# Down projection of a residual block in f32: one unit in six turns of each sweep by seven block products

## The chip, the cores and the metric

One core of a Trainium2 chip runs the whole kernel. The time is device microseconds of one execution. The kernel before takes 1611.67 us (median of 3 runs, 1611.58 to 1612.26).

## The reference, cut to what matters

```python
def conv_ffn(h, w_up, conv_w, w_down):
    ...
    return (jax.nn.gelu(gate, approximate=True) * val) @ w_down

def reference(x, ...):
    ...
    x = x + rms_norm(mix, ln_post_mix)
    h2 = rms_norm(x, ln_pre_ffn)
    x = x + rms_norm(conv_ffn(h2, w_up, conv_w, w_down), ln_post_ffn)
    return x
```

All is float32. There are 256 tokens, a model width of 2048 and an inner width of 8192, so the down projection is a product of 256x8192 with 8192x2048.

## The kernel before, in words

Every weight matrix is streamed once from HBM. A float32 product is made of three passes on TensorE: each operand is split into a rounded part `hi` (type fp32r) and the rest `lo`, and hi·hi, hi·lo and lo·hi are added in PSUM. ScalarE (ACT) makes `hi` with a copy that rounds, VectorE (DVE) makes `lo` with a subtraction, TensorE (PE) multiplies, SyncE (SP) issues the loads. Each engine runs a list of instructions that is written out by hand, in order, and semaphores tie the lists together.

The weights pass through `raw`, four slots of 128x2048 numbers (1 MB each, one load per slot, `load`, L282), and from there, in halves of 128x1024, through two rings of four places, `w_hi` and `w_lo` (`split`: L381 on ACT, L726 on DVE). Eight halves are a turn. In the down projection a half is one k tile (128 rows of `w_down`) by 1024 columns. Its 128x256 activations, a row of `ffT`, are split at the same time into `xs` (`split_xs`: L392 on ACT, L732 on DVE). `half_b` (L1320) then makes 12 matmuls of it: two tiles of 128 tokens, three passes, two column blocks of 512. There are two sweeps, one for each 1024 columns of the output, with 64 k tiles in 8 turns of 8 halves each. Sweep 0 adds up in PSUM banks 4 to 7, sweep 1 in banks 0 to 3. In the code the first turn of a sweep is written out and the others are a hardware loop (`down_turn`, L691 on ACT and L1191 on DVE); on PE the last turn is written out too, and in sweep 1 its last four halves are made by `last_halves` (L1334), tile by tile, so that the norm of the first tokens starts earlier.

What holds the order together around the change: ACT may write half h of turn m once `half_used` has reached 8m+h-3, that is when PE is through with the half that lay in the same ring place. DVE waits for `hi_ready` of the same half, PE for `lo_ready`. The load of slot s waits until `lo_ready` has reached 8m+2s-6, so slot 3 is loaded again when the whole turn before has been split.

At the boundary of the sweeps, in turn 0 of sweep 1, ACT squares the four finished banks of sweep 0 and DVE takes them out of PSUM (`sweep_out`). `actT`, 64 KB of each partition, holds the activations of the projections before and is used in the down projection only for what the squares write.

## Time and profile before

| | |
|---|---|
| median of 3 runs | 1611.67 us |
| the profiled execution, its own time | 1612.33 us |
| its span, first to last instruction | 1610.6 us |
| PE busy | 1600.2 us, 99% of the span |
| DVE busy | 1127.9 us, 70% |
| ACT busy | 791.1 us, 49% |
| DMA, share of 16 engines over the span | 61% |
| mean granted TensorE clock | 0.999 |

The span counts from the first to the last instruction; the execution's own time holds 1.7 us more around it. Busy times are of instructions; a matmul's time in the trace is longer than the distance to the next one, since they overlap. "PEld" is the load of the stationary operand, which runs beside the matmuls. An idle time is named with the engine and the line that ended it.

### The profile page before, as it was taken

What the parts mean: (1) busy time and instruction counts of PE and PEld (TensorE: products, weight loads), DVE (VectorE), ACT (ScalarE), POOL (GpSimd) and SP (SyncE); (2) the same over time, 40 slices, a digit from 0 to 9 for tenths busy, and PEclk for the clock granted to TensorE, in tenths of its full rate; (3) what the DMA queues carried; (4) which work ended last, traced back from release to release, by engine and by line L of the source; (5) the groups of instructions that cost most, each with busy time, mean ns of one, the idle gap of its engine ahead of it and who ended that gap; (6) DMA issues with size and microseconds to landing.
All of it is one profiled execution on the core that took longest, in us unless ns stands there. A gap on an engine that the chain in (4) does not pass through costs nothing.

```text
span 1610.6 us, 24829 instructions
## 1 busy us (share of the span) xinstructions
PE 1600.2 (99%) x8716; PEld 1384.2 (86%) x8716; DVE 1127.9 (70%) x1578; ACT 791.1 (49%) x1045; POOL 1.9 (0%) x12
## 2 busy tenths in 40 slices
PE   9999999999999999999999999999999999999998
PEld 7888888888888888888888888888888888888886
DVE  6556667677766787777777777777777755565555
ACT  6544544456555644444444444444444545554453
POOL 0000000000000000000000000000000000000000
PEclk9999999999999999999999999999999999999999
DMA  9885455556676465655655556556556666666662
GB/s 368 264 224 188 158 183 167 172 156 209 195 254 198 146 205 188 196 183 183 198 190 185 185 185 202 182 184 194 185 192 187 217 196 187 199 188 196 195 187 100
DMA packets 234788, 312.96 MB, mean 194 GB/s; under 512 B 5344, under 2 KB 209792, under 8 KB 233856
## 3 DMA queue, kind: packets, MB, share of 16 engines
q1 hardware_dynamic: 230912, 306.44, 59.6%
q10 hardware_dynamic: 3840, 6.05, 1.5%
q8 instruction: 23, 0.38, 0.1%
q14 instruction: 13, 0.11, 0.0%
HBM read 309.58 MB, written 2.88 MB: 194 GB/s over the span
## 4 chain that ended last, share of the span: by engine, by line
PE 99%; DMA 0%; DVE 0%; ACT 0%; SPq 0%; issue 0%; DVEq 0%
PE ps L1237 44%; PE ps L1328 26%; PE ps L1241 23%; PE ps L1376 3%; PE ps L1341 1%; PE ps L1252 1%; DMA raw<-in_w_in_dram 0%; PE ps L1257 0%; PE ps L1452 0%; PE ps L1470 0%; PE ps L1445 0%; PE ps L1460 0%; PE ps L1517 0%; DVE arena L1213 0%; PE ps L1281 0%; PE ps L1269 0%
## 5 line engine op out<-in xcount | busy, mean ns | idle before, releaser
L729 DVE TENSOR_TENSOR w_lo<-raw,w_hi 128x1024 fp32r<-128x1024 f32 x566 | 681.7, 1222 | 248.9 <-ACT w_hi L389 246.8
L389 ACT ACTIVATE w_hi<-raw 128x1024 fp32r<-128x1024 f32 x565 | 585.9, 1055 | 509.2 <-PE ps L1237 259.6
L1237 PE MATMUL ps<-actT,w_hi 128*128 128x512 f32 x3072 | 719.7, 390 | 0.0
L1237 PEld LDWEIGHTS ps<-actT,w_hi 128*128 128x128 f32 x3072 | 569.3, 188 | 115.5 <-issue 1.7
L1241 PEld LDWEIGHTS ps<-actT,w_lo 128*128 128x128 f32 x3072 | 383.2, 191 | 9.7 <-issue 1.4
L1241 PE MATMUL ps<-actT,w_lo 128*128 128x256 f32 x3072 | 388.9, 283 | 0.0
L1328 PE MATMUL ps<-w_hi,xs 128*128 128x512 f32 x1216 | 325.3, 389 | 0.0
L1328 PEld LDWEIGHTS ps<-w_hi,xs 128*128 128x128 f32 x1216 | 228.2, 188 | 47.3
L1328 PE MATMUL ps<-w_lo,xs 128*128 128x512 f32 x608 | 187.3, 389 | 0.0
L735 DVE TENSOR_TENSOR xs<-arena,xs 128x256 fp32r<-128x256 f32 x160 | 68.0, 425 | 169.4 <-ACT w_hi L389 169.1
L395 ACT ACTIVATE xs<-arena 128x256 fp32r (+1 forms) x160 | 66.7, 417 | 208.0 <-PE ps L1328 196.9
L1328 PEld LDWEIGHTS ps<-w_lo,xs 128*128 128x128 f32 x608 | 114.1, 188 | 23.8
L1141 DVE SCALAR_TENSOR_TENSOR arena<-arena,convw 128x256 f32<-128x256 f32 x256 | 106.9, 480 | 0.1
L740 DVE TENSOR_TENSOR arena<-ps,arena 128x512 f32<-128x512 f32 (+1 forms) x106 | 72.5, 684 | 1.6 <-ACT arena L402 1.6
L402 ACT ACTIVATE arena<-ps 128x512 f32<-128x512 f32 x106 | 61.4, 579 | 2.9 <-PE ps L1257 1.4
L1129 DVE TENSOR_TENSOR arena<-arena,rrow 128x512 f32<-128x512 f32 x64 | 44.3, 692 | 6.5
L1137 DVE TENSOR_SCALAR arena<-arena,convw 128x256 f32<-128x256 f32 x128 | 39.5, 351 | 8.9 <-DVE arena L1129 0.2
L1376 PE MATMUL ps<-w_hi,actT 128*128 128x512 f32 x128 | 32.5, 396 | 0.7 <-ACT w_hi L389 0.7
L1376 PEld LDWEIGHTS ps<-w_hi,actT 128*128 128x128 f32 x128 | 24.3, 192 | 6.4 <-issue 1.3
L568 ACT ACTIVATE arena<-ps 128x512 f32<-128x512 f32 x8 | 4.8, 597 | 35.3 <-PE ps L1460 35.3
L1171 DVE TENSOR_TENSOR arena<-arena 128x512 f32 (+1 forms) x32 | 22.0, 687 | 0.1
L674 ACT ACTIVATE arena<-arena 128x512 f32<-128x512 f32 x32 | 19.9, 622 | 1.1 <-DVE arena L1141 1.1
(132 smaller groups left out, 411.9 us busy)
## 6 DMA issues: line engine op xcount, KB each, us to landing
raw<-in_w_up_dram SPq DMA_DIRECT2D x128, 1024.0 KB, 5.5
raw<-in_w_down_dram SPq DMA_DIRECT2D x64, 1024.0 KB, 5.5
raw<-in_w_in_dram SPq DMA_DIRECT2D x58, 1024.0 KB, 5.2
raw<-in_w_o_dram SPq DMA_DIRECT2D x16, 1024.0 KB, 5.6
raw<-in_w_a_out_dram SPq DMA_DIRECT2D x8, 1024.0 KB, 5.2
raw<-in_w_b_out_dram SPq DMA_DIRECT2D x8, 1024.0 KB, 5.2
arena<-in_x_dram SPq DMA_DIRECT2D x1, 2048.0 KB, 17.3
arena<-in_x_dram ACTq DMA_DIRECT2D x2, 1024.0 KB, 6.6
```

The costliest lines, as they stand in the source:

```text
L389: act.activation(w_hi[:, h % RING, :], raw[:, h // 2, h % 2 * HALF:(h % 2 + 1) * HALF], ACT.Copy)\
L395: act.activation(xs[:, h % RING, 0, :], src, ACT.Copy)
L402: act.activation(lo_part, ps[:, bank:bank + 2, S:2 * S], ACT.Copy).then_inc(copied, 1)
L729: dve.tensor_tensor(w_lo[:, h % RING, :], raw[:, h // 2, h % 2 * HALF:(h % 2 + 1) * HALF], w_hi[:, h % RING, :].bitcast(F32), ALU.subtract ...
L735: dve.tensor_tensor(xs[:, h % RING, 1, :], src, xs[:, h % RING, 0, :].bitcast(F32), ALU.subtract)
L740: dve.tensor_tensor(dst, ps[:, bank:bank + 2, 0:S], lo_part, ALU.add).then_inc(summed, 1)
L1129: dve.tensor_tensor(src[:, :, 2:], src[:, :, 2:], rrow[:].unsqueeze(1).broadcast_to([P, 2, S]), ALU.mult)\
L1141: dve.scalar_tensor_tensor(out=dst[:, a, :], in0=src[:, a, i:i + S], scalar=w(i, a), in1=dst[:, a, :], op0=ALU.mult, op1=ALU.add).then_inc ...
L1237: return pe.matmul(ps[:, bank + c, :], w_hi[:, h % RING, at:at + P], actT[:, k, :, :].rearrange("p a s -> p (a s)"), start=start, stop=stop)
L1241: return pe.matmul(ps[:, bank + c, 0:S], w_lo[:, h % RING, at:at + P], actT[:, k, 0, :], start=start, stop=stop)
L1328: ins = pe.matmul(ps[:, bank + 2 * t + c, :], xpart[:, tokens], wpart[:, slot, c * 512:(c + 1) * 512], start=(first and xpart is x_hi and ...
L1376: ins = pe.matmul(ps[:, 4 + 2 * t + c, :], xpart[:, t * P:(t + 1) * P], wpart[:, slot, c * 512:(c + 1) * 512], start=(k == 0 and xpart is ...
```

## The change

In turns 1 to 6 of each sweep the last two halves (k tiles 8i+6 and 8i+7 of the turn, slot 3 of `raw`) are no longer multiplied with 24 matmuls. The 256x256 activations and the 256x1024 weights are taken as 2x2 blocks, and Strassen's scheme in Winograd's form makes the product of seven block products, each of three passes: 21 matmuls (`seven_products`, L1697 of the new kernel). The blocks and their sums are split into `hi` and `lo` in `forms`, which lies in `actT`, and in a small new tile `a_parts`; `convw`, `rrow` and `yn[sweep]` hold the sums.

- DVE makes seven sums (`sum_forms`) behind half 4 and the `lo` parts in eight subtractions (`rest_of_forms`) behind half 5. ACT rounds in `round_given` (four instructions) behind half 4 and in `round_sums` (four) behind half 5. ACT and DVE do not split halves 6 and 7 in these turns.
- PE waits for all of it (`lo_ready` at 8m+8) before the first of the 21 matmuls. Three of the seven products go into the banks of the sweep's sum (one each), four (P1, P5, P6, P7) into the other four banks, where they add up over the six turns. All 21 give `half_used` its 2 at the end.
- In the last turn of a sweep ACT copies P1 out of PSUM behind half 1 (`copy_p1`), and DVE adds P5, P6 and P7 to it behind half 3 (`sum_products`, four instructions). Sweep 0: the result is added to the sweep's banks by DVE in turn 0 of sweep 1, before ACT's squares, which now read it from SBUF and wait for it (`c_summed`); the multiplication by the gain moves behind half 5. Sweep 1: ACT rounds the result (`round_u`, behind its half 3), DVE makes the rest (`rest_of_u`, behind its half 5), and PE adds both to its banks with 8 matmuls by the identity (`add_products`) between half 3 of the last turn and `last_halves`.
- After a turn with seven products ACT may write halves 0 to 3 at other counts of `half_used` (`FREED`): 8m-3, 8m-2, 8m-5, 8m-4 in place of 8m-3 to 8m.
- The loops of ACT, DVE and PE now cover turns 2 to 5; turns 0, 1, 6 and 7 are written out.
- PE's waits for free banks move: `summed` from the start of sweep 1 to the start of turn 1 of sweep 0; new ones are `u_summed` at the start and `c_summed` at turn 1 of sweep 1.

The diff, cut (indentation taken off, empty lines left out):

```diff
+forms = actT[:].rearrange("p k a s -> p (k a s)")
+B1, B2, BT, BLK = 0, 512, 1536, 512
+b_hi, b_lo = forms[:, 0:7 * BLK], forms[:, 7 * BLK:14 * BLK]
+s_hi, s_lo = forms[:, 7168:7680], forms[:, 7680:8192]
+a_parts = sb("a_parts", [P, 2, 3 * P], F32R)
+a_hi, a_lo = a_parts[:, 0, :], a_parts[:, 1, :]
+s123 = convw[:].rearrange("p i t -> p (i t)")
+s4 = rrow[:, 0:P]
+u_hi, u_lo, ident_r = forms[:, 0:2048], forms[:, 2048:4096], forms[:, 4096:4096 + P]
...
+SUMS, HALVES_HI = 7, 7
+FREED = (-3, -2, -5, -4)
+def forms_at(sweep, i):
+    return (FF // P // 8 - 2) * sweep + i - 1
...
+def round_given(m, i):
+    act.wait_ge(raw_landed[3], 16 * m + 16)
+    act.wait_ge(half_used, 8 * m)
+    act.activation(b_hi[:, B2:BT], raw[:, 3, 2 * BLK:4 * BLK], ACT.Copy).then_inc(form_hi, 1)
+    act.activation(b_hi[:, B1:B2], raw[:, 3, 0:BLK], ACT.Copy).then_inc(form_hi, 1)
+    act.activation(a_hi[:, 0:S], ffT[:, 8 * i + 7, :], ACT.Copy).then_inc(form_hi, 1)
+    act.activation(a_hi[:, S:S + P], ffT[:, 8 * i + 6, 0:P], ACT.Copy).then_inc(form_hi, 1)
+def round_sums(sweep, i):
+    n = forms_at(sweep, i)
+    act.wait_ge(form_summed, SUMS * n + 2)
+    act.activation(b_hi[:, BT:BT + 2 * BLK], yn[sweep][:, 0, :], ACT.Copy).then_inc(form_hi, 1)
+    act.wait_ge(form_summed, SUMS * n + 6)
+    act.activation(s_hi[:, 0:3 * P], s123, ACT.Copy).then_inc(form_hi, 1)
+    act.activation(s_hi[:, 3 * P:4 * P], s4, ACT.Copy).then_inc(form_hi, 1)
+    act.wait_ge(form_summed, SUMS * n + 7)
+    act.activation(b_hi[:, BT + 2 * BLK:BT + 4 * BLK], yn[sweep][:, 1, :], ACT.Copy).then_inc(hi_ready, 2)
+def copy_p1(sweep, m):
+    act.wait_ge(half_used, 8 * m)
+    act.activation(yn[sweep][:, 0, 0:BLK], ps[:, 4 * sweep, :], ACT.Copy).then_inc(u_copied, 1)
+def round_u():
+    act.activation(ident_r, ident[:], ACT.Copy)
+    act.wait_ge(u_summed, 8)
+    for t in range(T):
+        act.activation(u_hi[:, t * SW:(t + 1) * SW], yn[1][:, t, :], ACT.Copy).then_inc(u_rounded, 1)
+def down_turn(sweep, i, with_forms=False, behind_forms=False, first=False, last=False):
     m = i + (N_DOWN // 8 + sweep * (FF // P // 8))
     if sweep == 0:
         act.wait_ge(ff_done, 4 * i + 4)
-    for h in range(8):
-        split_xs(m, h, ffT[:, 8 * i + h, :])
+    for h in range(6 if with_forms else 8):
+        split_xs(m, h, ffT[:, 8 * i + h, :], free=FREED[h] if behind_forms and h < RING else None)
         if first and sweep == 0 and h == 3:
             copy_out(G_END - 1, 2, N_DOWN)
             gelu_of(FF // GC - 1)
         if first and sweep == 1 and h == 3:
-            act.wait_ge(half_used, N_DOWN + FF // P)
             for t in range(T):
-                square(ps[:, 4 + 2 * t:6 + 2 * t, :], actT[:, 2 * t:2 * t + 2, :, :], SWEEP_FFN + t)
+                act.wait_ge(c_summed, t + 1)
+                square(yn[0][:, t, :], actT[:, 2 * t:2 * t + 2, :, :], SWEEP_FFN + t)
+        if with_forms and h == 4:
+            round_given(m, i)
+        if with_forms and h == 5:
+            round_sums(sweep, i)
+        if last and h == 1:
+            copy_p1(sweep, m)
+        if last and sweep == 1 and h == 3:
+            round_u()
+turns = FF // P // 8
 down_turn(0, 0, first=True)
 act.wait_ge(ff_done, FF // GC)
 act.dma_start(gain2, ln_post_ffn.partition_broadcast(P)).then_inc(small["gain2"], 16)
-with act.Fori(1, FF // P // 8) as i:
-    down_turn(0, i)
-load_root_table(2)
-down_turn(1, 0, first=True)
-with act.Fori(1, FF // P // 8) as i:
-    down_turn(1, i)
+for sweep in range(2):
+    if sweep == 1:
+        load_root_table(2)
+        down_turn(1, 0, first=True)
+    down_turn(sweep, 1, with_forms=True)
+    with act.Fori(2, turns - 2) as i:
+        down_turn(sweep, i, with_forms=True, behind_forms=True)
+    down_turn(sweep, turns - 2, with_forms=True, behind_forms=True)
+    down_turn(sweep, turns - 1, behind_forms=True, last=True)
...
+def sum_forms(sweep, m, i):
+    n = SUMS * forms_at(sweep, i)
+    quarters = raw[:, 3, :].rearrange("p (a b c) -> p a b c", a=2, b=2)
+    t13, t2, t4 = two(yn[sweep][:, 0, :]), yn[sweep][:, 1, 0:BLK], yn[sweep][:, 1, BLK:2 * BLK]
+    b21, b22 = raw[:, 3, 2 * BLK:3 * BLK], raw[:, 3, 3 * BLK:4 * BLK]
+    a11, a21 = ffT[:, 8 * i + 6, 0:P], ffT[:, 8 * i + 6, P:S]
+    a12, a22 = ffT[:, 8 * i + 7, 0:P], ffT[:, 8 * i + 7, P:S]
+    s1, s2, s3 = (s123[:, q * P:(q + 1) * P] for q in range(3))
+    dve.wait_ge(raw_landed[3], 16 * m + 16)
+    dve.tensor_tensor(s1, a21, a22, ALU.add).then_inc(form_summed, 1)
+    dve.tensor_tensor(t13, quarters[:, :, 1, :], quarters[:, 0, :, :], ALU.subtract).then_inc(form_summed, 1)
+    dve.wait_ge(form_summed, n + 1)
+    dve.tensor_tensor(s2, s1, a11, ALU.subtract).then_inc(form_summed, 1)
+    dve.tensor_tensor(s3, a11, a21, ALU.subtract).then_inc(form_summed, 1)
+    dve.wait_ge(form_summed, n + 2)
+    dve.tensor_tensor(t2, b22, yn[sweep][:, 0, 0:BLK], ALU.subtract).then_inc(form_summed, 1)
+    dve.wait_ge(form_summed, n + 3)
+    dve.tensor_tensor(s4, a12, s2, ALU.subtract).then_inc(form_summed, 1)
+    dve.wait_ge(form_summed, n + 5)
+    dve.tensor_tensor(t4, b21, t2, ALU.subtract).then_inc(form_summed, 1)
+def rest_of_forms(sweep, m, i):
+    n = HALVES_HI * forms_at(sweep, i)
+    def rest(lo, full, hi):
+        dve.tensor_tensor(lo, full, hi.bitcast(F32), ALU.subtract).then_inc(form_lo, 1)
+    dve.wait_ge(form_hi, n + 1)
+    rest(b_lo[:, B2:BT], raw[:, 3, 2 * BLK:4 * BLK], b_hi[:, B2:BT])
+    dve.wait_ge(form_hi, n + 2)
+    rest(b_lo[:, B1:B2], raw[:, 3, 0:BLK], b_hi[:, B1:B2])
+    dve.wait_ge(form_hi, n + 3)
+    rest(a_lo[:, 0:S], ffT[:, 8 * i + 7, :], a_hi[:, 0:S])
+    dve.wait_ge(form_hi, n + 4)
+    rest(a_lo[:, S:S + P], ffT[:, 8 * i + 6, 0:P], a_hi[:, S:S + P])
+    dve.wait_ge(form_hi, n + 5)
+    rest(b_lo[:, BT:BT + 2 * BLK], yn[sweep][:, 0, :], b_hi[:, BT:BT + 2 * BLK])
+    dve.wait_ge(form_hi, n + 6)
+    rest(s_lo[:, 0:3 * P], s123, s_hi[:, 0:3 * P])
+    dve.wait_ge(form_hi, n + 7)
+    rest(s_lo[:, 3 * P:4 * P], s4, s_hi[:, 3 * P:4 * P])
+    dve.wait_ge(hi_ready, 8 * m + 8)
+    dve.tensor_tensor(b_lo[:, BT + 2 * BLK:BT + 4 * BLK], yn[sweep][:, 1, :],
+                      b_hi[:, BT + 2 * BLK:BT + 4 * BLK].bitcast(F32), ALU.subtract).then_inc(lo_ready, 2)
+def sum_products(sweep):
+    u = yn[sweep]
+    p5, p6, p7 = (ps[:, 4 * sweep + q, :] for q in (1, 2, 3))
+    dve.wait_ge(u_copied, sweep + 1)
+    dve.tensor_tensor(u[:, 0, BLK:SW], p6, u[:, 0, 0:BLK], ALU.add).then_inc(u_summed, 1)
+    dve.wait_ge(u_summed, 4 * sweep + 1)
+    dve.tensor_tensor(u[:, 1, 0:BLK], p7, u[:, 0, BLK:SW], ALU.add).then_inc(u_summed, 1)
+    dve.tensor_tensor(u[:, 0, BLK:SW], p5, u[:, 0, BLK:SW], ALU.add).then_inc(u_summed, 1)
+    dve.wait_ge(u_summed, 4 * sweep + 2)
+    dve.tensor_tensor(u[:, 1, BLK:SW], p5, u[:, 1, 0:BLK], ALU.add).then_inc(u_summed, 1)
+def rest_of_u():
+    for t in range(T):
+        dve.wait_ge(u_rounded, t + 1)
+        dve.tensor_tensor(u_lo[:, t * SW:(t + 1) * SW], yn[1][:, t, :],
+                          u_hi[:, t * SW:(t + 1) * SW].bitcast(F32), ALU.subtract).then_inc(u_rest, 1)
+def down_turn(sweep, i, with_forms=False, first=False, last=False):
     m = i + (N_DOWN // 8 + sweep * (FF // P // 8))
-    for h in range(8):
+    for h in range(6 if with_forms else 8):
         split_xs(m, h, ffT[:, 8 * i + h, :])
         if first and sweep == 0 and h == 3:
             value_half(FF // GC - 1)
             product(FF // GC - 1)
         if first and sweep == 1 and h == 3:
+            dve.wait_ge(half_used, N_DOWN + FF // P)
+            for t in range(T):
+                dve.tensor_tensor(two(yn[0][:, t, :]), ps[:, 4 + 2 * t:6 + 2 * t, :], two(yn[0][:, t, :]),
+                                  ALU.add).then_inc(c_summed, 1)
+        if first and sweep == 1 and h == 5:
             dve.wait_ge(small["gain2"], 16)
             for t in range(T):
-                sweep_out(4, t, yn[0][:, t, :], gain2[:, 0:SW], sq_done, 5 * T + t + 2)
+                dve.wait_ge(sq_done, 5 * T + t + 2)
+                dve.tensor_tensor(yn[0][:, t, :], yn[0][:, t, :], gain2[:, 0:SW], ALU.mult).then_inc(sw_out, 1)
+        if with_forms and h == 4:
+            sum_forms(sweep, m, i)
+        if with_forms and h == 5:
+            rest_of_forms(sweep, m, i)
+        if last and h == 3:
+            sum_products(sweep)
+        if last and sweep == 1 and h == 5:
+            rest_of_u()
...
+def seven_products(m, c_bank, p_bank, first=False, last=False):
+    def a_given(at):
+        return a_hi[:, at:at + P], a_lo[:, at:at + P]
+    def a_sum(q):
+        return s_hi[:, q * P:(q + 1) * P], s_lo[:, q * P:(q + 1) * P]
+    def b(at):
+        return b_hi[:, at:at + BLK], b_lo[:, at:at + BLK]
+    pe.wait_ge(lo_ready, 8 * m + 8)
+    for (x_hi, x_lo), (y_hi, y_lo), bank, alone in (
+            (a_given(S), b(B1), p_bank, True),
+            (a_given(0), b(B2), c_bank, False),
+            (a_sum(3), b(B2 + BLK), c_bank + 1, False),
+            (a_given(P), b(BT + 3 * BLK), c_bank + 2, False),
+            (a_sum(0), b(BT), p_bank + 1, True),
+            (a_sum(1), b(BT + 2 * BLK), p_bank + 2, True),
+            (a_sum(2), b(BT + BLK), p_bank + 3, True)):
+        pe.matmul(ps[:, bank, :], x_hi, y_hi, start=(first and alone), stop=False)
+        pe.matmul(ps[:, bank, :], x_hi, y_lo, start=False, stop=False)
+        ins = pe.matmul(ps[:, bank, :], x_lo, y_hi, start=False, stop=(last and alone))
+    ins.then_inc(half_used, 2)
+def add_products():
+    pe.wait_ge(u_rest, T)
+    for bank in range(4):
+        for part in (u_hi, u_lo):
+            pe.matmul(ps[:, bank, :], ident_r, part[:, bank * BLK:(bank + 1) * BLK], start=False, stop=False)
 for sweep in range(2):
-    bank = 4 - 4 * sweep
+    bank, p_bank = 4 - 4 * sweep, 4 * sweep
     m = N_DOWN // 8 + sweep * turns
+    def turn_of_seven(i, first=False, last=False):
+        b_turn(i + m, bank, range(6))
+        seven_products(i + m, bank, p_bank, first, last)
     if sweep == 1:
+        pe.wait_ge(u_summed, 4)
+    b_turn(m, bank, range(8), first=True)
+    if sweep == 0:
         pe.wait_ge(summed, G_END)
-    b_turn(m, bank, range(8), first=True)
-    with pe.Fori(1, turns - 1) as i:
-        b_turn(i + m, bank, range(8))
+    else:
+        pe.wait_ge(c_summed, T)
+    turn_of_seven(1, first=True)
+    with pe.Fori(2, turns - 2) as i:
+        turn_of_seven(i)
+    turn_of_seven(turns - 2, last=True)
     b_turn(m + turns - 1, bank, range(8) if sweep == 0 else range(4), last=True)
+add_products()
 last_halves(N_END // 8 - 1)
```

**Where the instructions move.** DVE, turn 1 of sweep 0 (`w_lo` of half 5, the eight rests, and the first half of the next turn); before, this stretch held halves 5, 6 and 7, each of these two rows:

```order
L735 TENSOR_TENSOR xs<-arena,xs 128x256
L729 TENSOR_TENSOR w_lo<-raw,w_hi 128x1024 [waits hi_ready]
L734 REGISTER_ALU
L735 ISA [waits hi_ready]
L735 TENSOR_TENSOR xs<-arena,xs 128x256
L729 TENSOR_TENSOR w_lo<-raw,w_hi 128x1024 [waits hi_ready]
```

Now:

```order
L1278 TENSOR_TENSOR arena<-raw,arena 128x512 [waits form_summed]
L802 TENSOR_TENSOR xs<-arena,xs 128x256 [waits hi_ready]
L796 TENSOR_TENSOR w_lo<-raw,w_hi 128x1024 [waits hi_ready]
L1285 TENSOR_TENSOR actT<-raw,actT 128x1024 [waits form_hi]
L1285 TENSOR_TENSOR actT<-raw,actT 128x512 [waits form_hi]
L1285 TENSOR_TENSOR a_parts<-arena,a_parts 128x256 [waits form_hi]
L1285 TENSOR_TENSOR a_parts<-arena,a_parts 128x128 [waits form_hi]
L1285 TENSOR_TENSOR actT<-arena,actT 128x1024 [waits form_hi]
L1285 TENSOR_TENSOR actT<-convw,actT 128x384 [waits form_hi]
L1285 TENSOR_TENSOR actT<-rrow,actT 128x128 [waits form_hi]
L1302 TENSOR_TENSOR actT<-arena,actT 128x1024 [waits hi_ready]
```

The last row is the one that PE's seven products wait for. The row at the top is the last of the seven sums.

ACT, last turn of sweep 1, its halves 1 to 4. Before, these rows alternated without anything between the halves:

```order
L394 REGISTER_ALU
L395 ISA [waits half_used]
L395 ACTIVATE xs<-arena 128x256
L389 ACTIVATE w_hi<-raw 128x1024 [waits half_used,raw_landed1]
L395 ISA [waits half_used]
L395 ACTIVATE xs<-arena 128x256
L389 ACTIVATE w_hi<-raw 128x1024 [waits half_used,raw_landed1]
```

Now:

```order
L412 ACTIVATE w_hi<-raw 128x1024 [waits half_used,raw_landed0]
L737 ACTIVATE arena<-ps 128x512 [waits half_used]
L418 ACTIVATE xs<-arena 128x256 [waits half_used]
L412 ACTIVATE w_hi<-raw 128x1024 [waits half_used,raw_landed1]
L418 ACTIVATE xs<-arena 128x256 [waits half_used]
L412 ACTIVATE w_hi<-raw 128x1024 [waits half_used,raw_landed1]
L741 ACTIVATE actT<-ident 128x128
L744 ACTIVATE actT<-arena 128x1024 [waits u_summed]
L744 ACTIVATE actT<-arena 128x1024
L418 ACTIVATE xs<-arena 128x256 [waits half_used]
L412 ACTIVATE w_hi<-raw 128x1024 [waits half_used,raw_landed2]
```

Halves 4 to 7 of ACT (`raw_landed2` and on) stand behind a wait for DVE's sums, where they stood behind PE's progress alone.

DVE in the same turn, behind half 3:

```order
L1310 TENSOR_TENSOR arena<-ps,arena 128x512 [waits u_copied]
L1312 TENSOR_TENSOR arena<-ps,arena 128x512 [waits u_summed]
L1313 TENSOR_TENSOR arena<-ps,arena 128x512
L1315 TENSOR_TENSOR arena<-ps,arena 128x512 [waits u_summed]
L802 TENSOR_TENSOR xs<-arena,xs 128x256 [waits hi_ready]
L796 TENSOR_TENSOR w_lo<-raw,w_hi 128x1024 [waits hi_ready]
L802 TENSOR_TENSOR xs<-arena,xs 128x256 [waits hi_ready]
L796 TENSOR_TENSOR w_lo<-raw,w_hi 128x1024 [waits hi_ready]
L1320 TENSOR_TENSOR actT<-arena,actT 128x1024 [waits u_rounded] x2
```

The last row, two instructions, stands behind the splits of halves 4 and 5, and PE's eight matmuls by the identity wait for it.

## Rows read from the trace of the kernel before

**Rows 1.** The page: busy time of the engines, and shares of the chain of waits by line.

```profile
PE 1600.2 (99%) x8716; PEld 1384.2 (86%) x8716; DVE 1127.9 (70%) x1578; ACT 791.1 (49%) x1045; POOL 1.9 (0%) x12
...
PE ps L1237 44%; PE ps L1328 26%; PE ps L1241 23%; PE ps L1376 3%; PE ps L1341 1%; PE ps L1252 1%; DMA raw<-in_w_in_dram 0%; PE ps L1257 0%; PE ps L1452 0%; PE ps L1470 0%; PE ps L1445 0%; PE ps L1460 0%; PE ps L1517 0%; DVE arena L1213 0%; PE ps L1281 0%; PE ps L1269 0%
```

**Rows 2.** Chain of waits in order of time: start us, length us, engine, tile, line, count.

```profile
1254.84 337.28 PE ps L1328 x1488
```

**Rows 3.** Timeline, loop of sweep 0: start, length, engine, line, count, [idle before, releaser].

```profile
1327.66 1.07 PE L1328 MATMUL ps<-w_hi,xs 128*128 128x512 f32 x4
...
1328.42 0.42 ACT L395 ACTIVATE xs<-arena 128x256 fp32r x1 [1.35 <-PE ps L1328]
...
1328.75 1.05 ACT L389 ACTIVATE w_hi<-raw 128x1024 fp32r<-128x1024 f32 x1
...
1329.96 0.42 DVE L735 TENSOR_TENSOR xs<-arena,xs 128x256 fp32r<-128x256 f32 x1 [1.16 <-ACT w_hi L389]
...
1330.30 1.22 DVE L729 TENSOR_TENSOR w_lo<-raw,w_hi 128x1024 fp32r<-128x1024 f32 x1
```

**Rows 4.** 1300 to 1400 us: waits (us in total, times, longest), and loads (us to landing).

```profile
ACT xs L395 <- PE ps L1328: 49.9, 37, 1.3
DVE xs L735 <- ACT w_hi L389: 42.9, 37, 1.2
...
raw<-in_w_down_dram SPq DMA_DIRECT2D x19, 1024.0 KB, 5.5
```

**Rows 5.** Timeline of DVE, end of the up projection: instructions back to back.

```profile
1246.00 0.68 DVE L740 TENSOR_TENSOR arena<-ps,arena 128x512 f32<-128x512 f32 x1
1246.79 0.69 DVE L1129 TENSOR_TENSOR arena<-arena,rrow 128x512 f32<-128x512 f32 x1
...
1249.74 0.69 DVE L1171 TENSOR_TENSOR arena<-arena 128x512 f32 x1
1250.34 0.42 DVE L735 TENSOR_TENSOR xs<-arena,xs 128x256 fp32r<-128x256 f32 x1
1250.68 1.22 DVE L729 TENSOR_TENSOR w_lo<-raw,w_hi 128x1024 fp32r<-128x1024 f32 x1
1251.81 0.42 DVE L735 TENSOR_TENSOR xs<-arena,xs 128x256 fp32r<-128x256 f32 x1
```

**Rows 6.** Timeline of ACT in a turn of the gates: instructions back to back.

```profile
263.34 0.40 ACT L552 ACTIVATE arena<-arena 128x256 f32 x1
263.65 0.29 ACT L553 ACTIVATE arena<-arena 128x128 f32 x1
263.85 1.04 ACT L389 ACTIVATE w_hi<-raw 128x1024 fp32r<-128x1024 f32 x1
264.80 0.57 ACT L402 ACTIVATE arena<-ps 128x512 f32<-128x512 f32 x1
```

**Rows 7.** Timeline, turn 0 of sweep 1, which is written out: PE, ACT and DVE.

```profile
1436.46 1.07 PE L1328 MATMUL ps<-w_hi,xs 128*128 128x512 f32 x4
...
1437.11 0.42 ACT L395 ACTIVATE xs<-arena 128x256 fp32r<-128x256 f32 x1 [1.35 <-PE ps L1328]
1437.44 1.04 ACT L389 ACTIVATE w_hi<-raw 128x1024 fp32r<-128x1024 f32 x1
...
1438.52 0.43 DVE L735 TENSOR_TENSOR xs<-arena,xs 128x256 fp32r<-128x256 f32 x1 [1.16 <-ACT w_hi L389]
```

**Rows 8.** Timeline of the start: PE takes up after a wait for ACT.

```profile
8.52 1.06 ACT L389 ACTIVATE w_hi<-raw 128x1024 fp32r<-128x1024 f32 x1 [2.58 <-DMA raw<-in_w_in_dram]
...
9.69 1.46 PEld L1376 LDWEIGHTS ps<-w_hi,actT 128*128 128x128 f32 x7 [1.10 <-issue]
```

**Rows 9.** Windows behind the last matmul: stretch, length, busy of each engine, PEclk, DMA.

```profile
1602.80:1603.80 1.00, 0.20 (x1) 0.00 (x0) 0.88 (x5) 0.69 (x2) 0.00 (x0) 1.00 1.00 397
...
1607.20:1607.60 0.40, 0.00 (x0) 0.00 (x0) 0.16 (x1) 0.00 (x0) 0.00 (x0) 1.00 1.01 317
1607.60:1608.00 0.40, 0.00 (x0) 0.00 (x0) 0.00 (x0) 0.00 (x0) 0.00 (x0) 0.53 1.19 312
```

35 lines of the change are left out of this document (23 added, 12 removed).

## The prediction

> **What bounds the kernel now.** The page comes first: PE is busy for 99% of the span and the chain of waits is PE's own lines, with L1328, the down and output projections, at 26% [rows 1]. DVE has 30% of the span to spare, ACT 51%. Next the pace: 1488 matmuls of L1328 stand in the chain in 337.28 us [rows 2], 0.2267 us each. A half of 12 is then 2.72 us, a turn of 96 is 21.76 us.
>
> The timeline shows what follows what in the loop [rows 3]. PE's row is four matmuls, of which the last two open a new half, at 1327.66 + 2 x 0.227 = 1328.11. ACT starts 0.31 us after that, its second instruction 0.33 us later, and DVE starts 0.16 us after ACT's end at 1329.80. In turns that are written out these gaps are 0.20 (1436.91 to 1437.11) and 0.04 us [rows 7]. In each half ACT waits 1.35 us for PE and DVE 1.16 us for ACT [rows 4], so PE never waits. Only matmuls taken away can save time, and only while DVE and ACT stay ahead.
>
> **PE's matmuls.** Removed: 12 turns x 3 = 36 matmuls x 0.2267 = **8.16 us**. Added: `add_products`, 8 matmuls of the same 512 columns, **1.81 us**. Nothing else runs on PE.
>
> **DVE and ACT in a turn with seven products.** I need distances from start to start, which are 0.09 us shorter than the lengths. DVE back to back: 0.60 for 512 columns, 0.34 for 256, 1.13 for 1024 [rows 5]; the trace of before has no 128 or 384 of this kind beside others, and the line through these points gives 0.21 and 0.47. An instruction that needs the result of the one just before starts 0.11 after its end (1246.00 to 1246.79, length 0.68). ACT: 0.31 for 256, 0.20 for 128, 0.95 for 1024 [rows 6], about 0.52 for 512.
>
> Let 0 be PE's start of the turn. In the loop ACT may write half 4 when half 0 is used: 2.72 + 0.31 = 3.03, its `w_hi` ends at 3.03 + 0.33 + 1.05 = 4.41, DVE starts at 4.57. From there DVE is never free: half 4, 0.34 + 1.13 = 1.47; the seven sums, 4 x 0.21 + 1.13 + 2 x 0.60 = 3.17; half 5, 1.47; seven rests, 1.13 + 0.60 + 0.34 + 0.21 + 1.13 + 0.47 + 0.21 = 4.09; the last rest with its whole length, 1.22. The sum is 11.42, so `lo_ready` comes at **15.99**. PE ends half 5 at 6 x 2.72 = **16.32**. It takes up 0.11 us after what it waited for [rows 8], and the weight load must stand up to 0.2 us before the matmul, so 0 to 0.2 us are to spare in the loop and 0.23 more in turns 1 and 6. I take 0.05 us of wait in each of the 8 loop turns, **0.4 us**.
>
> ACT is covered: `round_given` follows half 4 from 4.31 to 6.3, half 5 to 7.6, and its last rounding, released by DVE's last sum at 9.3, is done at 10.4, where DVE wants it at 14.8. The load of slot 3 is released at 15.99, takes 5.5 us [rows 4], is in place 0.4 us into the next turn and is wanted 3.9 us later. Were DVE later than this, each of the 12 turns would pay, since ACT's half 4 is released by PE and the lateness comes again.
>
> **The boundary of the sweeps.** DVE's two additions and ACT's squares behind them come before half 4 of turn 0. ACT's half 3 is released at 0.2, DVE splits it by 3.3, adds until 5.6, ACT squares to 6.6 and then splits half 4, DVE has it at 9.6; PE wants it at 10.88. Nothing, with 1.3 us to spare.
>
> **The last turn.** In sweep 0 `copy_p1` and four sums (about 3 us) delay half 4 to 9.6, again in front of 10.88: nothing. In sweep 1 PE itself waits for the end of the chain, and all of it is in series. ACT copies P1 from 0.20, takes half 2 at 0.70 and half 3 from 1.98 to 3.36. DVE splits half 2 at 2.12 and half 3 at 3.59 (free at 5.06), and its four sums end at 5.06 + 0.80 + 2 x 0.60 + 0.69 = 7.75. ACT rounds from 7.85 (2 x 0.95), and only then splits half 4, from 9.75, done at 11.13, and half 5. DVE splits half 4 at 11.17, half 5 at 12.64, and makes the two rests from 14.11 to 14.11 + 1.13 + 1.22 = 16.46. PE has ended half 3 at 4 x 2.72 = 10.88 and can take up at about 16.65. That is a **wait of 5.8 us** on the bounding engine. `last_halves` behind it finds half 4 ready and halves 6 and 7 at 17.9 and 19.3, before it needs them.
>
> **The clock.** Behind the last matmul, which ends at 1603.0, the granted clock stays at 1.00 until 1607.6 and is at half after that [rows 9]: it fell 4.6 us after PE's last work, once. A wait of 5.8 us is longer, so I expect the 1.2 GHz level when PE takes up. No matmul of this trace runs at that level, so the price has bounds only: 0, and all 56 matmuls that are left, each 512 columns at 1.2 GHz = 0.427 instead of 0.227, 11.2 us. If the clock takes as long to come back as it took to fall, 4.6 x (1 - 0.227/0.427) = **2.1 us**; I take that, since rows 9 are all there is. The Trainium skill (TensorE: Matmul & The Clock Gate, Why this matters for your kernels) advises against idle stretches of TensorE between bursts of matmuls because the clock falls back to half; it speaks against this change, and by a rule without that the sum would be 2.1 us lower.
>
> **The sum**, against the profiled execution's 1612.33: - 8.16 + 1.81 + 0.4 + 5.8 + 2.1 = 1614.3. The median of the runs is 0.66 below that execution, so 1613.6. No change by measurement means within 0.2% of 1611.67, 1608.45 to 1614.89, about what a measurement of this kernel can tell.
>
> **Rivals.**
> - *The forecast*, 1613.6 (1612.5 to 1615.5): saving and last wait nearly cancel, the clock falls. Chance 0.42, of which 0.06 lie beyond 1614.89.
> - *The clock stays up.* One fall in the trace says little on when the next comes; the wait is only 1.2 us longer than that delay. Then 1611.5. Chance 0.20.
> - *DVE becomes the bound in the turns with seven products: slower.* DVE works 3.17 + 4.09 + 1.13 + 6 x 1.47 = 17.2 of 21.1 us there, and from 4.57 on in one row. It decides from 0.2 us on: 18 instructions in that row, each 0.03 us dearer than the line says (the 128s have no row, and loop turns have register work between short ones), are 0.5 us a turn, 6 us in 12, and 5.6 more than my 0.4: 1619.2. If instructions did not overlap at all, 17 x 0.09 = 1.5 us a turn; against that speaks the 1.13 of a 1.22 us instruction [rows 5]. Chance 0.26.
> - *The last wait is much shorter: faster.* It is the sum of 14 instructions and their gaps, and I see no way around any of them in the lists. If half of it went, the clock would stay up too: 1611.5 - 2.9 = 1608.6, and without it 1605.7. That PE's new matmuls run faster than 0.2267 us would do the same, by 0.01 us each over 252, 2.5 us. Chance 0.12, nearly all faster by over 0.2%.
>
> Faster: 0.11. Within 0.2%: 0.36 of the forecast, 0.20 and 0.01, 0.57. Slower: 0.06 + 0.26 = 0.32. The range reaches down to 1608.0, which leaves out most of the last rival, and up to 1619.5, which leaves out a third of DVE's, together under 2 in 10.
>
> **What the profile after should show.** 8688 matmuls instead of 8716 (-36 + 8). In the waits of PE one of 5 to 6 us for DVE's `rest_of_u`, and waits for `rest_of_forms` that are under 0.1 us each, if there at all; if these are 12 of 0.3 us or more, DVE is the bound. Turns of 21.1 us between 1276 and 1591. PEclk under 1.00 just behind the long wait, or 1.00 if the clock stays. DVE's busy time up by some 77 us from these turns: 12 times the lengths of the sums and rests, 3.8 + 5.9, less those of two halves, 3.3. If there is no long wait ahead of `add_products`, my chain through ACT's half 4 is wrong, and the time is near 1606.

## The result and the profile after

| | before | after |
|---|---|---|
| median of 20 runs each | 1611.97 us | 1614.55 us |
| lowest to highest | 1611.51 to 1612.95 | 1613.25 to 1617.44 |
| the profiled execution, its span | 1612.33, 1610.6 us | 1614.23, 1612.4 us |

The ratio is 1.0016, 95% interval 1.001 to 1.0023. The kernel after is slower by 2.6 us: the interval leaves out 1, so the loss is clear of noise, but it is small. The forecast was 1613.6, "within 0.2%" of the kernel before. The measured median lies in its range (1612.5 to 1615.5), 0.34 us from the 1614.89 above which the prediction called it slower. (One number ahead of the prediction is wrong and bears on nothing: `actT` has 16 x 2 x 256 x 4 bytes, 32 KB of each partition, not 64.)

The page of the kernel after, beside [rows 1]: busy times, and the chain of waits by line. L1388 and L1392 are the old L1237 and L1241, L1479 is the old L1328.

```profile
PE 1597.1 (99%) x8688; PEld 1380.4 (86%) x8688; DVE 1195.3 (74%) x1722; ACT 812.4 (50%) x1098; POOL 2.0 (0%) x12
...
PE ps L1388 44%; PE ps L1392 23%; PE ps L1479 21%; PE ps L1527 3%; PE ps L1492 1%; PE ps L1718 1%; PE ps L1719 1%; PE ps L1717 1%; PE ps L1403 1%; PE ps L1408 0%; DMA raw<-in_w_in_dram 0%; PE ps L1603 0%; PE ps L1621 0%; PE ps L1727 0%; PE ps L1596 0%; PE ps L1611 0%
```

PE makes 8688 matmuls as foreseen and is busy 3.1 us less, yet the span is 1.8 us longer: PE must wait somewhere. The waits of PE from 1240 us on (line, releaser, us in total, times, longest) are a single one:

```profile
PE ps L1727 <- DVE actT L1320: 5.3, 1, 5.3
```

That is `add_products` waiting for `rest_of_u` in the last turn. There is no wait for `rest_of_forms`. The chain in the loop of sweep 0 (start, length, line, count), beside [rows 2]:

```profile
1297.36 16.32 PE ps L1479 x72
...
1318.54 16.32 PE ps L1479 x72
...
1339.71 16.32 PE ps L1479 x72
```

Six halves take 16.32 us as predicted, and the turns follow each other by 21.18 us instead of 21.08. So the 21 products between take 4.86 us, 0.2314 each, where `half_b` needs 0.2267.

One loop turn, whose first matmul starts at 1339.55 in the timeline (the chain shows it 0.16 us later; columns as in [rows 3]):

```profile
1342.58 0.42 ACT L418 ACTIVATE xs<-arena 128x256 fp32r x1 [3.70 <-PE ps L1479]
...
1344.12 0.42 DVE L802 TENSOR_TENSOR xs<-arena,xs 128x256 fp32r<-128x256 f32 x1 [3.08 <-ACT w_hi L412]
...
1345.60 0.28 DVE L1268 TENSOR_TENSOR convw<-arena 128x128 f32 x1
...
1348.75 0.41 DVE L802 TENSOR_TENSOR xs<-arena,xs 128x256 fp32r<-128x256 f32 x1
...
1350.22 1.81 DVE L1285 TENSOR_TENSOR actT<-raw,actT 128x1024 fp32r<-128x1024 f32 x2
...
1353.63 0.54 DVE L1285 TENSOR_TENSOR actT<-convw,actT 128x384 fp32r<-128x384 f32 x1
...
1354.10 0.28 DVE L1285 TENSOR_TENSOR actT<-rrow,actT 128x128 fp32r<-128x128 f32 x1
1354.31 1.21 DVE L1302 TENSOR_TENSOR actT<-arena,actT 128x1024 fp32r<-128x1024 f32 x1
...
1355.87 0.40 PE L1717 MATMUL ps<-actT,a_parts 128*128 128x512 f32 x1
```

DVE starts 4.57 us into the turn and is never free until L1302 ends at 1355.52, 15.97 us in (predicted: 4.57 and 15.99). PE starts its products at 16.32. The two sizes that had no row stand at the distances that the line through the others gave: 0.47 for 384 columns (1353.63 to 1354.10), 0.21 for 128.

The last turn of sweep 1, in which PE starts at 1573.69 and is through with half 3 at 1584.57:

```profile
1578.72 0.68 DVE L1310 TENSOR_TENSOR arena<-ps,arena 128x512 f32<-128x512 f32 x1
...
1581.36 2.01 ACT L744 ACTIVATE actT<-arena 128x1024 fp32r<-128x1024 f32 x2 [4.17 <-DVE arena L1315]
1583.27 0.40 ACT L418 ACTIVATE xs<-arena 128x256 fp32r<-128x256 f32 x1
...
1584.66 0.42 DVE L802 TENSOR_TENSOR xs<-arena,xs 128x256 fp32r<-128x256 f32 x1 [3.33 <-ACT w_hi L412]
...
1587.61 2.35 DVE L1320 TENSOR_TENSOR actT<-arena,actT 128x1024 fp32r<-128x1024 f32 x2
...
1590.02 3.78 PE L1727 MATMUL ps<-actT 128*128 128x512 f32 x8 [5.28 <-DVE actT L1320]
...
1593.59 0.79 PE L1492 MATMUL ps<-w_hi,xs 128*128 128x512 f32 x2
```

It is the predicted series. ACT splits half 4 only behind the two roundings, DVE splits halves 4 and 5 only behind ACT, and `rest_of_u` stands behind both. It ends 16.27 us into the turn (predicted 16.46), and PE has lost 1590.02 - 1584.57 = 5.45 us. The eight matmuls then take 3.57 us, 0.446 each. Why, the windows tell (stretch, length, busy of each engine, PEclk, DMA):

```profile
1586.00:1587.00 1.00, 0.00 (x0) 0.00 (x0) 1.00 (x3) 1.00 (x2) 0.00 (x0) 1.00 0.00 0
1587.00:1588.00 1.00, 0.00 (x0) 0.00 (x0) 1.00 (x2) 1.00 (x3) 0.00 (x0) 0.55 0.00 0
...
1592.00:1593.60 1.60, 1.60 (x6) 1.21 (x5) 0.90 (x1) 0.00 (x0) 0.00 (x0) 0.50 0.00 0
1593.60:1594.00 0.40, 0.40 (x3) 0.34 (x2) 0.00 (x0) 0.00 (x0) 0.00 (x0) 0.59 0.00 0
```

The granted clock fell to half (1.2 GHz) at about 1587.1, 2.4 us behind PE's last matmul, and came back at about 1593.9. PE worked 3.9 us at the lower level. Against the steady distance of 0.2267 us this is 3.57 - 1.81 in `add_products` and 0.17 behind it, 1.93 us. Some 0.14 of it is not the clock: in the run with the wait filled, below, the same eight matmuls take 1.95 us at full clock.

The account of the two profiled executions: - 8.16 + 1.81 + 5.45 (wait) + 1.93 (clock) + 1.18 (products, 252 x 0.0047) = + 2.21. The start was 0.42 us shorter in this one (ACT's first `w_hi` came earlier), which leaves 1.79 of the 1.8 us between the spans.

### The profile page after: what moved, and what is told of

Same layout as the page of the kernel before. It is cut to its first block, busy times and chain, and to the rows that moved or that the text cites. A ratio compares the mean times of both kernels' runs of the same rounds, so it can differ in the third digit from the quotient of the medians.

```text
span 1612.4 us, 24809 instructions
## 1 busy us (share of the span) xinstructions
PE 1597.1 (99%) x8688; PEld 1380.4 (86%) x8688; DVE 1195.3 (74%) x1722; ACT 812.4 (50%) x1098; POOL 2.0 (0%) x12
## 4 chain that ended last, share of the span: by engine, by line
PE 98%; DVE 1%; DMA 0%; ACT 0%; SPq 0%; issue 0%; DVEq 0%; ACTq 0%
PE ps L1388 44%; PE ps L1392 23%; PE ps L1479 21%; PE ps L1527 3%; PE ps L1492 1%; PE ps L1718 1%; PE ps L1719 1%; PE ps L1717 1%; PE ps L1403 1%; PE ps L1408 0%; DMA raw<-in_w_in_dram 0%; PE ps L1603 0%; PE ps L1621 0%; PE ps L1727 0%; PE ps L1596 0%; PE ps L1611 0%
## 5 line engine op out<-in xcount | busy, mean ns | idle before, releaser
L796 DVE TENSOR_TENSOR w_lo<-raw,w_hi 128x1024 fp32r<-128x1024 f32 x542 | 652.1, 1221 | 248.1 <-ACT w_hi L412 246.1
L412 ACT ACTIVATE w_hi<-raw 128x1024 fp32r<-128x1024 f32 x541 | 560.6, 1055 | 509.2 <-PE ps L1388 259.6
L1388 PE MATMUL ps<-actT,w_hi 128*128 128x512 f32 x3072 | 719.7, 390 | 0.0
L1388 PEld LDWEIGHTS ps<-actT,w_hi 128*128 128x128 f32 x3072 | 569.3, 188 | 115.5 <-issue 1.7
L1392 PEld LDWEIGHTS ps<-actT,w_lo 128*128 128x128 f32 x3072 | 383.2, 191 | 9.7 <-issue 1.4
L1392 PE MATMUL ps<-actT,w_lo 128*128 128x256 f32 x3072 | 388.9, 283 | 0.0
L1479 PE MATMUL ps<-w_hi,xs 128*128 128x512 f32 x1024 | 275.9, 389 | 0.0
L1479 PEld LDWEIGHTS ps<-w_hi,xs 128*128 128x128 f32 x1024 | 192.2, 188 | 39.8
L1479 PE MATMUL ps<-w_lo,xs 128*128 128x512 f32 x512 | 157.7, 389 | 0.0
L418 ACT ACTIVATE xs<-arena 128x256 fp32r<-128x256 f32 (+1 forms) x136 | 56.0, 412 | 166.8 <-PE ps L1479 155.7
L802 DVE TENSOR_TENSOR xs<-arena,xs 128x256 fp32r<-128x256 f32 x136 | 57.3, 421 | 99.8 <-ACT w_hi L412 99.7
L1479 PEld LDWEIGHTS ps<-w_lo,xs 128*128 128x128 f32 x512 | 96.1, 188 | 20.0
L1285 DVE TENSOR_TENSOR actT<-raw,actT 128x1024 fp32r<-128x1024 f32 (+1 forms) x24 | 21.8, 948 | 0.0
```

Of the source, the lines that this page charges most:

```text
L412: act.activation(w_hi[:, h % RING, :], raw[:, h // 2, h % 2 * HALF:(h % 2 + 1) * HALF], ACT.Copy)\
L418: act.activation(xs[:, h % RING, 0, :], src, ACT.Copy)
L796: dve.tensor_tensor(w_lo[:, h % RING, :], raw[:, h // 2, h % 2 * HALF:(h % 2 + 1) * HALF], w_hi[:, h % RING, :].bitcast(F32), ALU.subtract ...
L802: dve.tensor_tensor(xs[:, h % RING, 1, :], src, xs[:, h % RING, 0, :].bitcast(F32), ALU.subtract)
L1388: return pe.matmul(ps[:, bank + c, :], w_hi[:, h % RING, at:at + P], actT[:, k, :, :].rearrange("p a s -> p (a s)"), start=start, stop=stop)
L1392: return pe.matmul(ps[:, bank + c, 0:S], w_lo[:, h % RING, at:at + P], actT[:, k, 0, :], start=start, stop=stop)
```

## The experiments

All ratios compare with the kernel before on the same chip (medians 1611.89 to 1611.94 us in the timed ones). The changed kernel's 1614.55 us was measured beside a median of 1611.97, so the chips differ by under 0.1 us. What I wanted to know: whether the clock's price is real and apart from the wait's; whether the last wait hangs on the order of the lists; how near DVE is to bounding the loop; and why the products stand 0.2314 us apart.

### The wait filled with matmuls

PE works through its last wait on matmuls that nobody needs.

```diff
+pe.wait_ge(u_summed, 8)
+for _ in range(30):
+    pe.matmul(ps[:, 4, 0:3 * P], a_hi[:, 0:P], a_hi[:, 0:3 * P], start=True, stop=True)
 pe.wait_ge(u_rest, T)
```

> The changed kernel with 30 matmuls of 384 columns (a_parts by itself, into a PSUM bank that nobody reads any more) ahead of PE's wait for rest_of_u in the last turn. They last about 5.2 us, so PE waits about as long as before, but works while it waits. My theory (the clock falls in the wait, and PE's next 3.9 us run at 1.2 GHz): the granted clock stays at 1.00 through the end, add_products takes 1.8 instead of 3.6 us, the time is 1.9 us lower, near 1612.6, and the runs scatter less, as those of the kernel before do, because where the clock falls and rises differs from run to run. Rival (the low clock costs nothing, since DVE sets the end there): no change from 1614.5, same scatter.

Measured: 1612.25 us (1611.93 to 1612.94, 11 runs), ratio 1.0003, interval 0.9993 to 1.0012. Timeline and window of this kernel:

```profile
1589.87 2.11 PE L1730 MATMUL ps<-actT 128*128 128x512 f32 x8
```
```profile
1584.00:1590.00 6.00, 5.92 (x34) 5.53 (x33) 5.49 (x7) 4.25 (x7) 0.00 (x0) 1.00 0.00 0
```

`add_products` starts as late as in the changed kernel, but at full clock it is 1.6 us shorter (1.95 us to the next matmul, at 1591.82, in place of 3.57). The whole kernel is 2.3 us faster than the changed one, with 30 matmuls more: the clock costs about 2 us by itself. The mean granted clock of an execution is 0.996 or 0.997 in all 20 runs of the changed kernel and 0.998 or 0.999 in all 11 of this one. The runs lie within 1.0 us here and within 4.2 us in the changed kernel, but that the clock makes this scatter is not shown: 19 of the changed kernel's 20 runs lie within 2.5 us, and the run ordered by pass, below, in which the clock falls too, lies within 1.2.

### Half of the wait filled

The same with `range(15)`.

> As the changed kernel, with 15 matmuls of 384 columns on PE ahead of its wait for rest_of_u (30 in the run with the gap filled). They take about 2.7 us, so PE idles the other 2.7 us of the wait. They write a bank that is not used any more, so the output does not change. Theory (the last wait costs what it costs only through the clock, since the wait is in both): the clock fell 2.4 us after PE's last matmul in the changed kernel and 4.6 to 5.2 us after it in others, so with 2.7 us of idle it falls in some executions and not in others. Median between 1612.3 (never, as with the gap filled) and 1614.5 (always, as the changed kernel), with a scatter of over 1.5 us among the runs. Rival (any idle stretch at all brings the fall and the whole price): 1614.5 in nearly all runs.

Measured: 1613.78 us (1612.32 to 1614.49, 11 runs), ratio 1.0011, interval 1.0002 to 1.002; three runs lie at 1612.3 to 1612.8, eight at 1613.8 to 1614.5. So the fall comes in some executions and not in others, as expected, if the two groups are those with and without it; the only profiled one, 1613.78, had it. PE's 15 matmuls end at 1587.10, `add_products` starts at 1589.78:

```profile
1590.20:1591.00 0.80, 0.80 (x5) 0.67 (x4) 0.80 (x1) 0.00 (x0) 0.00 (x0) 1.00 0.00 0
1591.00:1592.00 1.00, 1.00 (x4) 0.76 (x3) 1.00 (x3) 0.00 (x0) 0.00 (x0) 0.53 0.00 0
```

The clock fell at about 1591.1, 4 us behind the last of the 15, when PE had been at work again for 1.3 us. So in this execution the price of 2.7 us of idleness was paid after the idle stretch was over.

### The order of the lists in the last turn

Two versions. In the first, one line of DVE's list moves: `rest_of_u` behind half 3.

```diff
-if last and sweep == 1 and h == 5:
+if last and sweep == 1 and h == 3:
     rest_of_u()
```

> One line moved in the changed kernel: in the last turn of sweep 1 DVE makes rest_of_u behind half 3 and its sums, in front of half 4, where it stood behind half 5. ACT's order is as in the changed kernel. Theory (the last wait is the series of DVE's instructions between the sums and rest_of_u): rest_of_u starts when ACT has rounded, near 7.8 + 1.0 after the turn's start, and ends by 11.3 with PE through half 3 at 10.9, so the wait of 5.4 us shrinks to 0.3 to 0.8 us and the clock stays at full speed: 1614.5 - 4.9 - 1.9 = 1607.7, range 1606.9 to 1608.8. Half 4 is then split 2.9 us later on DVE, done near 12.8, where PE wants it at 11.3 + 1.8 = 13.1; if that cover fails PE waits up to 1 us more at the first half of last_halves: up to 1609. Rival (ACT's rounding behind the sums is what holds it, and half 4 behind that): a wait of over 2 us stays, 1610 or more.

Measured: 1606.97 us (1606.55 to 1607.69, 7 runs), ratio 0.997, interval 0.9959 to 0.9981. Its timeline:

```profile
1582.55 2.36 DVE L1320 TENSOR_TENSOR actT<-arena,actT 128x1024 fp32r<-128x1024 f32 x2 [1.13 <-ACT actT L744]
...
1584.97 2.11 PE L1727 MATMUL ps<-actT 128*128 128x512 f32 x8
...
1586.91 0.61 PE L1492 MATMUL ps<-w_hi,xs 128*128 128x512 f32 x2
```

PE loses 0.3 us where it lost 5.45, the clock stays at 1.00, and the cover of half 4 holds. The changed kernel becomes 7.6 us faster by one line.

In the second, PE's matmuls move instead, and both other lists round later:

```diff
-if last and sweep == 1 and h == 3:
+if last and sweep == 1 and h == 5:
     round_u()
-if last and sweep == 1 and h == 5:
+if last and sweep == 1 and h == 7:
     rest_of_u()
...
 for h in range(4, 8):
     ins = tile(0, h, (0, 1))
+ins = add(1, (0, 1))
 ins.then_inc(tile0_done, 1)
+add(2, (2, 3))
 for h in range(4, 8):
     ins = tile(1, h, (0,))
...
```

Here `add` is `add_products` for the rows it has to wait for and its banks: the eight matmuls stand together, behind the four halves of the first 128 tokens and ahead of those of the second.

> The changed kernel with the last turn reordered: ACT rounds the summed products behind its half 5 instead of half 3, DVE makes the rests behind half 7 instead of half 5, and PE adds them behind the four halves of the first 128 tokens (banks 0 and 1, then 2 and 3) instead of ahead of them, so PE has 5.4 us more of work before it needs them. Theory (the last wait and the clock behind it are what gives the saving back): the wait of 5.3 us goes or is under 0.5 us, the clock stays at 1.00, the time is 5.4 + 1.9 = 7.3 us lower, about 1607.3, which is 4.7 us or 0.3% below the kernel before. Rival (the wait moves to halves 6 and 7, which ACT and DVE now make later): 2 us or more of wait for lo_ready in the last turn, 1609 or more.

Measured: 1606.54 us (1606.41 to 1607.09, 6 runs), ratio 0.9967, interval 0.9955 to 0.9979. PE has no wait in the last turn. What is left against the kernel before is - 5.17 by the account (- 8.16 + 1.81 + 1.18), - 5.4 measured.

### More work on DVE in each turn with seven products

Two subtractions of 128 columns, each of which waits for the one ahead, stand in front of the last two rests. They add 0.52 us to DVE's row.

```diff
+for q in range(2):
+    ...
+    dve.tensor_tensor(rrow[:, P:S], ffT[:, 8 * i + 7, 0:P], a_hi[:, 0:P].bitcast(F32),
+                      ALU.subtract).then_inc(more_done, 1)
```

> The changed kernel with two more subtractions of 128 columns on DVE in each of the 12 turns with seven products, ahead of the seventh rest, each waiting for the one before it (their result is not used): some 0.65 to 0.8 us of DVE work a turn. In the changed kernel the last rest ends 0.35 us before PE's first product in a loop turn and 0.6 us before it in turn 6, and PE takes up 0.04 to 0.11 us after what it waits for. If DVE's list is the next bound (my theory): PE waits about 0.7 - 0.25 = 0.45 us in each of 8 loop turns and 0.2 us in the 4 others, some 4.5 us in all, 1619. Rival (a wait in one turn is made up in the next, since ACT and DVE run ahead): one wait at most, 1615.

Measured: 1617.31 us (1616.71 to 1617.62, 6 runs), ratio 1.0033, interval 1.0021 to 1.0045. That is 2.8 us over the changed kernel, less than expected, since the pair was also shorter than assumed. The timeline of a loop turn, and the chain (the starts of two turns):

```profile
1354.71 0.60 DVE L1303 TENSOR_TENSOR rrow<-arena,a_parts 128x128 f32<-128x128 f32 x2
...
1356.71 0.50 PE L1723 MATMUL ps<-actT,a_parts 128*128 128x512 f32 x1
```
```profile
1318.82 2.73 PE ps L1485 x12
...
1340.32 2.73 PE ps L1485 x12
```

A turn is 21.50 us instead of 21.18, and the chain now runs through DVE's rests in every loop turn. Of the 0.52 us, 0.32 appear: DVE has 0.20 us to spare in the changed kernel. Part of the 0.32 is PE's start behind a wait, in which the second product comes 0.33 us behind the first (1356.71 to 1357.04) where it is 0.23 otherwise. Eight loop turns of 0.32 are 2.6 of the 2.8 us. Once it is late, the lateness comes again in each turn, as the prediction had it for its third rival.

### Seven products in sweep 0 alone

In sweep 1 every turn is of 96 matmuls again, and `add_products` with all that leads to it is gone.

> Seven products in sweep 0 alone. Sweep 1 runs as in the kernel before, so copy_p1, sum_products, round_u, rest_of_u and add_products of sweep 1 are gone and with them the last wait. Theory (the turns with seven products gain 3 matmuls each, less 0.0047 us on each of their 21, the start is 0.4 us earlier, and the rest of the loss sits at the end): 18 x 0.2267 - 126 x 0.0047 + 0.4 = 3.9 us under the kernel before, 1608.0, range 1607.7 to 1608.8; no wait of PE over 0.3 us in the last turn, and turns of 21.18 us in sweep 0, 21.76 in sweep 1. Rival (the boundary of the sweeps, which I costed at nothing, loses time, or DVE is late in the loop): a wait of PE by L1749 or for c_summed, and over 1609.5.

Measured: 1608.63 us (1608.39 to 1609.01, 11 runs), ratio 0.998, interval 0.9971 to 0.9989: - 3.3 us, near the 3.5 of the matmuls alone (the shorter start was one execution's). The chain from the end of the last turn with seven products on:

```profile
1403.43 184.96 PE ps L1485 x816
1588.39 10.89 PE ps L1498 x48
```

816 matmuls at 0.2267 us without a break, over the boundary of the sweeps: what DVE and ACT do there for the seven products costs nothing, as I had put it. (PE's wait for `c_summed` is not in this run; the changed kernel has it, and its trace shows no wait of PE there either.) All of the loss sits in the last turn and in the distance of the products.

### Why the products stand 0.2314 us apart

First guess: three matmuls in a row into one bank. The order was turned round, all hi by hi first, so that each goes to another bank than the one ahead.

```diff
+for x, y in ((0, 0), (0, 1), (1, 0)):
+    for xs_of, ys_of, bank, alone in seven:
+        ins = pe.matmul(ps[:, bank, :], xs_of[x], ys_of[y], ...)
```

> The changed kernel with the 21 matmuls of the seven products ordered by pass (all hi.hi, then all hi.lo, then all lo.hi) instead of by product, so each matmul goes to another PSUM bank and another stationary block than the one before it. In the changed kernel they stand 0.2314 us apart, those of half_b 0.2267. Theory A (three matmuls in a row into the same bank, then a switch, make the 0.005 us): 0.2267 us, 12 x 21 x 0.0047 = 1.2 us less. Theory B (it is where the operands lie: the moving ones come from actT, not from the rings): 0.2314 as before, no change of the time. I hold B likelier, because the column passes of last_halves also stay in one bank for matmuls in a row and stand 0.2267 apart.

Measured: 1614.47 us (1614.03 to 1615.21, 11 runs), ratio 1.0017, interval 1.0008 to 1.0026, and turns of 21.21 us, 0.232 between products: no shorter than before. It is not the bank. Second guess: the variety of the operands.

```diff
-(a_given(0), b(B2), c_bank, False),
-...
+(a_given(S), b(B2), c_bank, False),
+...
```

> All seven products use the same pair of blocks (a_given(S) and b(B2)) in place of seven different pairs, in the same banks and the same order of passes, so that the down projection is not the reference's in these turns. Only the distance from one matmul to the next inside seven_products is asked for (0.2314 us in the changed kernel, 0.2267 in half_b). If the variety of the operands' addresses makes it longer, it falls to 0.227 and a turn is 21.08 us; if it is the place of the operands (actT and a_parts in place of w_hi and xs) or their shape, it stays at 0.231 and a turn at 21.18. The last wait and the time stay those of the changed kernel, 1613 to 1616.

Measured: 1614.59 us in one run; the chain has turns starting at 1318.40 and 1382.10, three turns of 21.23 us, so 4.90 us for 21 products, 0.2333 each. Not the variety: with `a_parts` as the only stationary operand it is even more. So the places were measured by themselves, with 48 matmuls behind `last_halves`. This run and the two like it are single executions, of which only distances are read:

```diff
+for x, y in triples(*split, *ring):      # xs, w_hi and w_lo
+    pe.matmul(ps[:, 4, :], x, y, start=True, stop=True)
+for x, y in triples(*parts, *ring):      # a_parts, w_hi and w_lo
+    ...
+for x, y in triples(*split, *block):     # xs, actT
+    ...
+for x, y in triples(*parts, *block):     # a_parts, actT
+    ...
```

> The changed kernel with 48 matmuls of 512 columns put on PE behind last_halves, which nobody waits for and which write an unused bank, so that the output does not change. They stand in four groups of 12, each in the pattern of seven_products (hi by hi, hi by lo, lo by hi, one bank): first stationary from xs and moving from w_hi and w_lo (as half_b), then stationary from a_parts, then stationary from xs with moving from actT, then stationary from a_parts with moving from actT (as seven_products). Asked for is the distance from start to start, 0.2267 us in half_b and 0.2314 us in seven_products. If the place of the stationary operand costs the 0.0047 us, groups 2 and 4 are at 0.231; if the place of the moving one, groups 3 and 4; if neither (the engines working beside it, or the list's own neighbours), all four are at 0.227 there, and if the pattern of passes does it, all four at 0.231. PE ends some 10.9 us later, while the norms and the stores behind last_halves take 6 to 7 us, so the time is about 1618.

Measured: 1618.58 us. Its chain of waits behind `last_halves`:

```profile
1605.50 2.72 PE ps L1760 x12
1608.21 2.80 PE ps L1762 x12
1611.01 2.75 PE ps L1764 x12
1613.76 2.80 PE ps L1766 x12
```

12 matmuls take 2.72 us (0.2267 each) from `xs` and 2.80 (0.2333) from `a_parts`: it is the stationary operand, whatever the moving one. (The third group, `xs` with `actT`, reads 2.75; it reads 2.72 in the next run, so the moving operand is not the cause there.) Next, the same kernel with the tile declared elsewhere.

```diff
 xs = sb("xs", [P, RING, 2, S], F32R)
+a_parts = sb("a_parts", [P, 2, 3 * P], F32R)
...
-a_parts = sb("a_parts", [P, 2, 3 * P], F32R)
```

> The kernel with the four groups of 12 matmuls, with the tile a_parts declared behind xs instead of last, nothing else. In the run before, the chain gave 2.72 us for stationary xs with moving w_hi and w_lo, 2.80 for stationary a_parts with the same moving tiles, 2.75 for xs with moving actT, 2.80 for a_parts with actT. As declared last, a_parts begins 103216 bytes behind the end of xs if tiles lie one behind the other, no multiple of 32 bytes; moved, it begins at a multiple of 1024 bytes, with the same shape and the same distance between its rows. If the address makes the stationary load slow, group 2 falls from 2.80 to 2.72 and group 4 to 2.75, and the products' turn in the loop from 21.18 us to 21.13 or less; if the shape of a_parts does it, groups 2 and 4 stay at 2.80. Time about 1618.

Measured: 1617.08 us, and the same rows read:

```profile
1604.17 2.72 PE ps L1760 x12
1606.89 2.72 PE ps L1762 x12
1609.61 2.72 PE ps L1764 x12
1612.33 2.72 PE ps L1766 x12
```

```profile
1605.38 2.72 PE ps L1760 x12
1608.10 2.80 PE ps L1762 x12
1610.89 2.75 PE ps L1764 x12
1613.64 2.80 PE ps L1766 x12
```

The turns of the loop are of 21.18 us again. It is the 64 bytes and not how far up the tile lies. A matmul of 512 columns whose stationary operand begins there takes 0.0067 us more in a row of its kind. Only 9 of the 21 products take theirs from `a_parts`, which makes 0.06 of the 0.10 us that a turn loses; the rest must fall on the matmuls among and behind them, as in the third group above. By the Trainium skill (SBUF — State Buffer, Operand start alignment) an operand in fp32 may begin at any multiple of 4 bytes; all three places are allowed by that, and what they cost is what these runs show.

Last, the better place in the faster kernel:

> The kernel whose add_products stand behind last_halves' tile and whose ACT and DVE lists round later (1606.54 us, no wait in the last turn), with a_parts declared behind xs. If a_parts' address makes its matmuls slow, the 12 x 9 products with a stationary operand from it gain up to 0.0067 us each, 0.4 to 0.7 us: 1606.0 (1605.7 to 1606.3). If not, 1606.5, unchanged.

Measured: 1605.67 us (1605.37 to 1605.76, 5 runs), ratio 0.996, interval 0.9947 to 0.9974. The chain in the loop:

```profile
1318.45 16.32 PE ps L1479 x72
...
1339.53 16.32 PE ps L1479 x72
```

A turn is 21.08 us. The time is just below my range, 0.9 us less than without the move, because I had counted nine products of each turn and the whole 0.10 us went. The kernel is 6.3 us faster than the one before: 36 - 8 matmuls of 0.2267 us are 6.35. With the list reordered and the tile moved, the change gives all that its matmuls are worth. This version is faster than the kernel before and the changed one.

## Why the prediction was right, and where it was not

- **The sum.** Predicted on top of - 8.16 + 1.81: 0.4 + 5.8 + 2.1 = 8.3 us. Found: 0 + 5.45 + 1.93 + 1.18 = 8.56. That the total is so near is in part luck: three terms were too high by 0.92 us together, and one that the sum did not have, the distance of the products, made 1.18. The mechanism, a saving nearly cancelled by one wait in the last turn and the clock behind it, is what the runs show. The medians differ by 2.6 us and not by the forecast's 1.9, which left the time near the upper bound of "within 0.2%".
- **PE's matmuls.** The count was right. The step that failed is "I take 0.2267 for the same 512 columns": the 252 products stood 0.2314 apart, 1.18 us. I had named such a deviation only on the fast side (0.01 us each). The cause, the first byte of a new tile, stood in the diff for anyone who adds up the tiles, but no row that I read in the trace of before shows such a case.
- **Waits in the loop.** I took 0.05 us in each of 8 turns; there were none. The room was given as 0 to 0.2 us, and the run with more work on DVE found 0.20. The slower rival, with a chance of 0.26 the largest after the forecast, was that near: 0.2 us of a turn of 21.
- **The last turn.** The wait was 5.45 us, not 5.8. `rest_of_u` ended 0.19 us earlier, and PE took up 0.06 us behind it instead of 0.19. The series was right, shown by its removal: with one line moved, the wait is 0.3 us. Wrong was the sentence of the fourth rival that I saw "no way around any of them in the lists". The changed kernel keeps this order, so the rival did not come; but the way around was one line.
- **The clock.** The price, 2.1, was near that measured, 1.8 to 1.9 in one execution and 2.3 between medians. The timing behind it was not, so the price was in part luck: the fall came 2.4 us behind the last matmul and not 4.6, the clock was back after 3.9 us of work and not 4.6, and in the run with half of the wait filled the fall came when PE worked again. The Trainium skill's advice against idle stretches between bursts (TensorE: Matmul & The Clock Gate, Why this matters for your kernels) is borne out here, since 2 of the kernel's 2.6 us of loss are the clock alone. The rival in which the clock stays up was given 1611.5; the filled run shows its real worth, 1612.25. The products add 1.18 us to it, the two waits that were put too high take off 0.75, and the kernel before was 0.25 us slower than the 1611.67 that I started from.
- **The boundary of the sweeps, ACT, the loads.** Costed at nothing, and nothing: 816 matmuls without a break in the run with sweep 0 alone, and loads of `w_down` in 5.6 us.
- **DVE's busy time** rose by 67 us in all, and not by 77 from the turns with seven products alone: a loop turn has 17.37 us of it, where one before had 12.49, so 12 turns make 59. The step was lengths added up; busy time counts instructions that overlap once. The 17.2 us that the third rival worked with, from distances, were near the 17.37.

## What to carry to other kernels

A saving that sits in a loop is given back at the one place where the bounding engine must wait for a chain of the others: before a change is judged, each engine's list there is to be read for work that stands in front of what is waited for and is needed later. Such a wait costs more than its length when the clock falls behind it: 2 us on top of 5.4 here. And where many matmuls take their stationary operand from a small tile, its first byte should be looked at: a tile declared last, behind others of odd sizes, cost 0.003 to 0.007 us per matmul here.

## What the runs showed of the hardware

- Stationary operand 64 bytes past a multiple of 128: 2.80 us for 12 fp32r matmuls of 512 columns, 2.72 on a multiple, in two runs against one, whether the tile lay at byte 127680 or 226240 of the partition. Only remainders of 0 and 64 were tried. Groups right behind, whose operands all lie on multiples, read 2.75 where the group ahead was slow and 2.72 where it was not; what they share is open. `half_a` (L1252 before, L1403 after) stands at 0.230 us (8 matmuls in 1.84 to 1.86 in the kernel before) with all its operands on multiples of 128, so there is another cause of the same size, which was not looked for.
- The granted clock falls 2.4 us (kernel after), 2.9 (more work on DVE), 4.0 (half filled), 4.6 (before) and 5.2 us (by pass) behind the last matmul, so one execution says little on when it falls in the next. It was back 3.3 to 4.7 us after PE had taken up work again.
